# Sample attention of a hybrid decoder step in four 32-column strips, with a token-major norm and separate semaphores for key and value pages

## What is computed

```
def attn_sample(q, k, v, k_past, v_past, lam):
    s_past = jnp.einsum("bqhnd,bkhnd->bhnqk", q, k_past) * scale
    s_new = jnp.einsum("bqhnd,bkhnd->bhnqk", q, k) * scale      # causal among the 8 new tokens
    w = softmax(concat(s_past, s_new))[:, :, 0] - lam * softmax(...)[:, :, 1]
    return einsum(w[..., :p], v_past) + einsum(w[..., p:], v)
o = rmsnorm(o, subln) * (1.0 - lam_init)
```

## Time and profile before

| | us |
|---|---|
| median of three runs (3421.71 to 3428.89) | 3424.6 |
| the profiled execution: its own time | 3428.04 |
| its span | 3426.4 |
| TensorE busy | 3235.2 (94% of the span) |
| VectorE busy | 1520.3 (44%) |
| ScalarE busy | 1083.0 (32%) |
| mean granted TensorE clock | 0.955 |

### The profile page before, as it was taken

How to read it: one execution, slowest core, us unless ns; L and a number is a source line. 1 busy time by engine, 2 the same in 40 slices (tenths; PEclk the granted TensorE clock), 3 DMA queues, 4 the chain that set the end, 5 groups by cost and what they waited for, 6 DMA issues and landing times.

```text
span 3426.4 us, 56080 instructions
## 1 busy us (share of the span) xinstructions
PE 3235.2 (94%) x21279; PEld 2959.4 (86%) x21279; DVE 1520.3 (44%) x1994; ACT 1083.0 (32%) x1287; POOL 29.7 (1%) x55
## 2 busy tenths in 40 slices
PE   7899987997789999999999989999989999999998
PEld 2588853775778998998998989999989999999998
DVE  1534574113653443443433564445554444444443
ACT  1322233103333323323323333333343333333332
POOL 0000000000000000000000000000000000000000
PEclk8999996877899999999999989999999999999999
DMA  9777777662347557557567534444434444444443
GB/s 347 243 246 249 236 267 261 226 239 80 100 146 247 179 179 245 177 184 246 167 193 243 161 114 150 151 147 149 148 116 149 151 147 148 151 147 149 151 147 110
DMA packets 512217, 624.17 MB, mean 182 GB/s; under 512 B 22416, under 2 KB 408081, under 8 KB 511444
## 3 DMA queue, kind: packets, MB, share of 16 engines
q1 hardware_dynamic: 504576, 595.68, 54.5%
q0 software_dynamic: 6112, 22.84, 1.8%
q10 hardware_dynamic: 1430, 4.24, 0.4%
HBM read 617.13 MB, written 5.54 MB: 182 GB/s over the span
## 4 chain that ended last, share of the span: by engine, by line
PE 88%; DVE 4%; DMA 4%; ACT 1%; issue 1%; SPq 0%; POOL 0%; POOLq 0%; DVEq 0%; ACTq 0%
PE mm L1417 80%; PE aux L1417 7%; DMA wide_first<-in_ada_mix_w 2%; DMA vpage<-in_cache_v 2%; PE mm L1510 1%; DVE a_rr L1201 1%; DVE l_g L1308 0%; SPq L362 0%; ACT tmp L613 0%; DVE a_qn L1204 0%; DVE pj L1212 0%; DVE p_s L1228 0%; DVE a_t L1210 0%; DVE rstd L898 0%; DVE a_t L1208 0%
## 5 line engine op out<-in xcount | busy, mean ns | idle before, releaser
L844 DVE TENSOR_TENSOR w_lo<-raw,w_hi 128x1024 fp32r<-128x1024 f32 x752 | 920.2, 1226 | 1431.2 <-ACT w_hi L526 1429.4
L526 ACT ACTIVATE w_hi<-raw 128x1024 fp32r<-128x1024 f32 x752 | 795.4, 1059 | 1724.8 <-PE mm L1417 1724.8
L1417 PE MATMUL mm<-h_hi,w_hi 128*128 128x320 f32 x3712 | 1164.6, 314 | 54.2 <-DVE h_lo L940 32.3
L1417 PE MATMUL mm<-h_hi,w_lo 128*128 128x320 f32 x3712 | 1151.4, 310 | 0.0
L1417 PE MATMUL mm<-h_lo,w_hi 128*128 128x320 f32 x3712 | 1151.3, 310 | 0.0
L1417 PEld LDWEIGHTS mm<-h_hi,w_hi 128*128 128x128 f32 x3712 | 701.5, 189 | 135.8 <-issue 133.2
L1417 PE MATMUL mm<-u_hi,w_hi 128*128 128x320 f32 x2304 | 712.0, 309 | 0.0
L1417 PE MATMUL mm<-u_hi,w_lo 128*128 128x320 f32 x2304 | 711.9, 309 | 0.0
L1417 PE MATMUL mm<-u_lo,w_hi 128*128 128x320 f32 x2304 | 711.9, 309 | 0.0
L1417 PEld LDWEIGHTS mm<-h_lo,w_hi 128*128 128x128 f32 x3712 | 701.7, 189 | 2.2 <-issue 2.2
L1417 PEld LDWEIGHTS mm<-h_hi,w_lo 128*128 128x128 f32 x3712 | 701.1, 189 | 0.0
(11 more groups left out here) (247 smaller groups left out, 1448.2 us busy)
## 6 DMA issues: line engine op xcount, KB each, us to landing
raw<-in_mlp_w SPq DMA_DIRECT2D x512, 512.0 KB, 3.6
narrow<-in_ada_mlp_w SPq DMA_DIRECT2D x256, 256.0 KB, 3.6
raw<-in_w_in_odd SPq DMA_DIRECT2D x96, 512.0 KB, 3.6
raw<-in_w_in_even SPq DMA_DIRECT2D x80, 512.0 KB, 6.6
wide_first<-in_ada_mix_w SPq DMA_DIRECT2D x64, 512.0 KB, 8.8
narrow<-in_ada_mix_w SPq DMA_DIRECT2D x128, 256.0 KB, 3.7
wide_later<-in_ada_mlp_w SPq DMA_DIRECT2D x64, 512.0 KB, 6.0
wide_later<-in_ada_mix_w SPq DMA_DIRECT2D x64, 512.0 KB, 5.2
```

The costliest lines, as they stand in the source:

```text
L526: fn(w_hi[:, slot], raw[:, slot], ACT.Copy).then_inc(hi_ready, 1)
L844: v.tensor_tensor(w_lo[:, slot], raw[:, slot], w_hi[:, slot].bitcast(F32), ALU.subtract).then_inc(lo_ready, 1)
L1417: return nc.tensor.matmul(out, lhsT, rhs, start=first, stop=last)
```

## The change

It does these things:

1. **Scores in strips.** `s_q` is now [128, 8 heads, 32]: for head h = 2j + a the 16 query columns stand at column 16a of its 32, the rest is zero. Head h goes to the PSUM strip 32j, and the two heads of a strip add into it, so the rows of the scores keep their order. The stationary operand has 32 columns in place of 128. The matmuls on the new keys move ahead of `fold`, next to those on the past keys.
2. **Values in strips.** The weights `s_pt` are now stationary, 32 columns for four samples, and the value pages move, 128 columns a head. Head 4*half + j goes to strip 32j; the result in `aux[:, 0, :]` is token-major and adds up over the four samples of a group. Since the columns of the other samples must be zero, VectorE clears the eight of the sample before. `s_pt` moves to a place that was `ktok`, and VectorE clears it first, behind a wait for `stored`.
3. **Token-major norm.** ScalarE squares the four 128 x 128 blocks of the result with a running sum, takes the roots; VectorE multiplies; TensorE turns the four blocks back (`s_back`); VectorE puts them into `pj` behind the second head of the prompt's norm and only then counts `s_out`. The head norm runs on 256 columns instead of 320.
4. **Own semaphores.** Keys count `keys_in`, values `values_in`. The keys of sample b wait for the transposes of sample b - 2 (`s_kTt` >= 2b - 2), only the values for `s_o` >= b - 1. TensorE waits for `values_in` ahead of the values.

```diff
-                if b >= 2:
-                    pool.wait_ge(s_o, b - 1)
...
+                if b >= 2:
+                    pool.wait_ge(s_kTt, 2 * b - 2)
+                for g in range(PAGES):
+                    pool.dma_start((kpage, kpage2)[b % 2][:, g, :],
...
+                                   ).then_inc(keys_in[b % 2], 16)
                 if b >= 2:
                     pool.wait_ge(s_o, b - 1)
                 for g in range(PAGES):
...
+                    pool.dma_start((vpage, vpage2)[b % 2][:, g, :],
...
+                                   ).then_inc(values_in[b % 2], 16)
...
             act.wait_ge(s_o, NB)
-            fn(pj[:, 0:H, SEQ:T], aux[:, 0, :].rearrange("p (h t) -> p h t", h=H), ACT.Copy).then_inc(s_out, 1)
-            act.wait_ge(s_out, 1)
+            for n in range(4):
+                ins = fn(s_kT[:, n // 2, P * (n % 2):P * (n % 2) + P], aux[:, 0, P * n:P * n + P], ACT.Square,
+                         accum_out=small[:, 1, 8 + n:9 + n])
+            ins.then_inc(s_sq, 1)
+            act.wait_ge(s_sq, 1)
+            fn(small[:, 1, 12:16], small[:, 1, 8:12], ACT.Sqrt, scale=1.0 / DV, bias=C("eps")).then_inc(s_root, 1)
...
-            step(v.memset(s_q[:, :], 0.0))
+            step(v.memset(s_q[:, :, :], 0.0))
+            dve.wait_ge(stored, 64)
+            step(v.memset(s_pt[:, :, :, :], 0.0))
...
                 if b:
                     dve.wait_ge(s_o, b)
+                    v.memset(s_pt[:, :, :, before:before + 8], 0.0)
...
+            dve.wait_ge(s_root, 1)
+            step(v.reciprocal(small[:, 1, 12:16], small[:, 1, 12:16]))
+            settle()
+            v.tensor_tensor(s_kT[:, 2:4, :].rearrange("p a (n d) -> p (a n) d", n=2),
+                            aux[:, 0, :].rearrange("p (n d) -> p n d", n=4),
+                            small[:, 1, 12:16].unsqueeze(2).broadcast_to([P, 4, P]), ALU.mult).then_inc(s_norm, 1)
             for i in range(H):
...
+                if i == 1:
+                    dve.wait_ge(s_back, 1)
+                    for n in range(4):
+                        rows, cols = slice(4 * (n % 2), 4 * (n % 2) + 4), slice(SEQ + 32 * (n // 2), SEQ + 32 * (n // 2) + 32)
+                        ins = v.tensor_scalar(pj[:, rows, cols], mm[:, 0, 0, P * n:P * n + P].rearrange("p (j t) -> p j t", j=4),
+                                              subln[:, 0:1], None, ALU.mult)
+                    ins.then_inc(s_out, 1)
...
-                for h in range(H):
-                    mul(mm[:, 2, 0, 0:PAST], s_q[:, P * h:P * h + P], s_kT[:, h, :], h == 0, h == H - 1)
+                for a in range(2):
+                    for j in range(4):
+                        h = 2 * j + a
+                        mul(mm[32 * j:32 * j + 32, 2, 0, 0:PAST], s_q[:, h, :], s_kT[:, h, :], a == 0, a == 1)
...
                 pe.wait_ge(s_pte, b + 1)
-                for h in range(H):
-                    out, cols, w = aux[:, 0, 64 * h + 8 * b:64 * h + 8 * b + 8], slice(P * h, P * h + P), slice(8 * h, 8 * h + 8)
-                    mul(out, page[:, 0, cols], s_pt[:, 0, w], True, False)
-                    mul(out, page[:, 1, cols], s_pt[:, 1, w], False, False)
-                    ins = mul(out, vtok[0:TS, 2, cols], s_pt[0:TS, 2, w], False, True)
+                pe.wait_ge(values_in[b % 2], 32 * (b // 2 + 1))
+                for half in range(2):
+                    for k in range(3):
+                        rows = P if k < 2 else TS
+                        keys = page[:, k, :] if k < 2 else vtok[0:TS, 2, :]
+                        for j in range(4):
+                            h = 4 * half + j
+                            at_col = 256 * (b // 4) + P * half
+                            ins = nc.tensor.matmul(aux[32 * j:32 * j + 32, 0, at_col:at_col + P], s_pt[0:rows, k, h, :],
+                                                   keys[:, P * h:P * h + P], start=b == half == k == 0,
+                                                   stop=b == NB - 1 and k == 2, skip_group_check=True)
```

More of the change, by code:

```diff
@@ L232, in trunk_kernel @@
         s_kT = at("s_kT", RM, [P, H, PAST])
-        s_q = at("s_q", RM + 8192, [P, H * (P + 16)])
+        s_q = at("s_q", RM + 8192, [P, H, 32])
         s_s = at("s_s", RM + 12800, [P, T])
-        s_pt = at("s_pt", RM + 14080, [P, 3, 64])
+        s_pt = at("s_pt", RH + 8192, [P, 3, H, 32])
         l_x2 = at("l_x2", RM, [P, 2, T])
@@ L477, in _ @@
                     pool.wait_ge(stored, 64)
+                pages = []
+                for g in range(PAGES):
+                    n = b * PAGES + g
+                    pages.append(pool.value_load(ptab[0:1, n:n + 1], min_val=0, max_val=A["cache_k"].shape[1] - 1))
+                if b >= 2:
+                    pool.wait_ge(s_kTt, 2 * b - 2)
+                for g in range(PAGES):
+                    pool.dma_start((kpage, kpage2)[b % 2][:, g, :],
+                                   A["cache_k"][0, bass.ds(pages[g], 1)].rearrange("o p h d -> p (o h d)")
+                                   ).then_inc(keys_in[b % 2], 16)
                 if b >= 2:
@@ L480, in _ @@
                 for g in range(PAGES):
[L481 to L485, removed]
+                    pool.dma_start((vpage, vpage2)[b % 2][:, g, :],
+                                   A["cache_v"][0, bass.ds(pages[g], 1)].rearrange("o p h d -> p (o h d)")
+                                   ).then_inc(values_in[b % 2], 16)
             pool.wait_ge(s_out, 1)
@@ L761, in _ @@
             act.wait_ge(o_ready, H)
+            act.wait_ge(s_out, 1)
             def mixed(n):
@@ L1274, in s_keys @@
                     half = slice(DH * n, DH * n + DH)
-                    ins = v.tensor_copy(s_q[half, :].rearrange("p (h c) -> p h c", h=H)[:, :, 8 * n:8 * n + DS],
-                                        pj[half, 0:H, SEQ + DS * b:SEQ + DS * b + DS])
+                    for a in range(2):
+                        at_col = 16 * a + 8 * n
+                        ins = v.tensor_copy(s_q[half, a:H:2, at_col:at_col + DS],
+                                            pj[half, a:H:2, SEQ + DS * b:SEQ + DS * b + DS])
                 ins.then_inc(s_prep, 1)
@@ L1677, in _ @@
             pe.wait_ge(mod_ready, F.now)
+            pe.wait_ge(s_norm, 1)
+            for n in range(4):
+                ins = turn(mm[:, 0, 0, P * n:P * n + P], s_kT[:, 2 + n // 2, P * (n % 2):P * (n % 2) + P])
+            ins.then_inc(s_back, 1)
             for i in range(H):
@@ L1681, in _ @@
                     pe.wait_ge(o_root, i - 1)
-                mul(mm[:, 2, i % 2, 0:T], C("ones"), l_g[:, 0, i % 2], True, True).then_inc(o_ms, 1)
+                mul(mm[:, 2, i % 2, 0:SEQ], C("ones"), l_g[:, 0, i % 2, 0:SEQ], True, True).then_inc(o_ms, 1)
             pe.wait_ge(gate_in, 64)
```

33 lines of the change are left out of this document (20 added, 13 removed).

## The result

| | before | after |
|---|---|---|
| median, us | 3426.74 (4 runs, 3421.71 to 3429.55) | 3339.58 (4 runs, 3338.09 to 3341.93) |
| ratio | | 0.9749, 95% from 0.9734 to 0.9765 |
| profiled execution, us | 3428.04, span 3426.4 | 3340.85, span 3339.1 |
| granted TensorE clock, mean | 0.955 | 0.966 |
| sample attention, first scores to the end of the last burst | 605.38 to 814.6, 209.2 us | 607.04 to 719.6, 112.6 us |

A forecast was written before the change was run, and what follows sets the result against it. It took one loop, TensorE's sample plus a page load that cannot start earlier, as the bound. From 3428.0 us, less 79.5 for the stage, 0 behind it and half of 3.4, came 3347 us, range 3325 to 3385.

The forecast's parts named there:

- What bounds it now: Sample attention, 209 us for eight samples: bound by one loop, TensorE's sample plus a page load that cannot start earlier.
- Strips at once: Scores and values: four strips run at once, past-key scores 1.0 us, new-key scores 0.5, values 2.2 at full clock.
- The end of 5.8 us: Values in strips: 5.8 us if each record took the 0.12 us of the new-key scores before the change.
- rivals 2 and 3: Strips not running at once, about 3393 us, chance 0.05; each strip draining before the next, about 3570, chance 0.02.
- TensorE's sample: TensorE's steps for one sample of the attention stage, summed: 11.5 us at full clock, 20.3 at half clock.
- The clock: Sample attention: granted clock taken as 0.7, between full and half clock, so a TensorE sample takes 15.6 us.
- Rival 1: Sample attention: clock stays at 0.50, TensorE bounds each sample at 20.3 us, about 3380 us in all; chance 0.25.
- Own semaphores: Sample attention: the transposes' wait of 1.87 us for key pages goes in each of seven samples; adaLN chunks are late next.
- What the stage takes: Sample attention: 42.5 MB of chunks and pages plus start, tail and gaps; ends at 735 instead of 814.6, gain 79.5 us.
- I add 10 us: Sample attention: an allowance for gaps between loads, since TensorE takes chunks in bursts and the ring holds one group.
- At 370 GB/s: Sample attention: the rate assumed for the 42.5 MB of loads, which gives 115 us.
- Behind the stage: After sample attention: +3 us before the first head, heads at 2.15 us each, sum 0; gates' weights covered by 5 us.

The follow-up runs named there:

- x2: The kernel before with only `s_q` at 32 columns per head and both kinds of scores in strips ahead of `fold`: 3424.31 us, ratio 1.0005.
- x1: The kernel before with only the semaphores and the order of the page loads changed, all matmuls as before: 3417.31 us, ratio 0.998.
- x3: The changed kernel, but the keys of sample b wait for `s_o` >= b - 1 again, as the values do: 3356.59 us, ratio 0.9815.
- x4: The changed kernel with `s_q` and the scores as before, values in strips and own semaphores kept: 3347.81 us, ratio 0.9786.
- x5: The changed kernel without the 12 value page loads of samples 2 to 7, earlier pages multiplied again: 3320.64 us, ratio 0.9685.

## Why the prediction was right, point by point

**What bounds it now: right in the main.** A loop of TensorE's steps and a page load that starts too late. It is not TensorE's whole sample, as the prediction has it: the scores lie beside the load. x2 shows that (shorter scores alone give nothing), x1 shows the load (earlier pages alone give 13 us in the stage), and x3 and x4 price the two inside the change at 16 and 9. Alone they are worth 13 and 0, together with the value strips 96.6, and the value strips are the largest part (x3, x4).

**Strips at once: right.** Scores 1.1 us against a summed 1.5, values 2.1 against 2.2. The end of 5.8 us that the range held for the values, and rivals 2 and 3, fall with it.

**TensorE's sample: a little too high.** 11.5 us at full clock had been summed; sample 0 takes 9.4. Of the 2.1 us, 1.0 is `fold`, which sample 0 doesn't have, and 0.4 are scores. It costs nothing in the time, since the DMA is the longer.

**The clock: between the forecast's cases, nearer to its good end.** I took 0.7 and a TensorE sample of 15.6. The stage was granted 0.90. Windows of after behind its longest waits for `wide_later`, and between two of them:

```profile
630.00:640.00 10.00, 9.49 (x61) 5.88 (x62) 1.95 (x7) 1.25 (x3) 0.00 (x0) 0.51 1.04 399
...
657.00:664.00 7.00, 5.25 (x54) 2.41 (x52) 0.00 (x0) 0.00 (x0) 0.00 (x0) 0.52 1.05 390
664.00:687.00 23.00, 19.83 (x226) 11.10 (x218) 7.69 (x27) 4.55 (x8) 4.21 (x8) 1.00 1.04 395
688.00:694.00 6.00, 5.10 (x22) 1.89 (x26) 0.48 (x3) 0.00 (x0) 0.00 (x0) 0.50 1.05 387
```

The clock fell three times, each time behind such an idle stretch of TensorE: 3.4 us, 1.8 and 1.7 us one after the other, and 2.7 us. In x5, the same matmuls with no idle stretch over 1.2 us from the first scores to the last burst, it was never below 1.00. Rival 1, half clock throughout, falls with that. The Trainium skill, "TensorE: Matmul & The Clock Gate", section "HAM oscillation", has a kernel that is throttled at every wait for DMA, with waits longer than its bursts. The trace agrees for the longest waits here and not for the short ones.

**Own semaphores: right, the price in part by luck.** The transposes no longer wait, and the adaLN chunk is what is late next. The price of 7 x 1.9 us, 13, is x1's 12.6, but the trace of before has six such waits of TensorE, 10.4 us in all, since the first sample's transposes (611.7) have none.

**What the stage takes: the term that was mis-sized.** 42.5 MB at 370 GB/s plus 4, 4 and 10 us was to end at 735; it ended at 719.6. Two parts of the term failed, both to the same side. "I add 10 us" for gaps: there were none (DMA share 1.00). "At 370 GB/s": the steady part ran at 385 to 403, so the middle samples took 16.1 us on average instead of 17 to 18. 369 was the mean of 30 to 55 us of before; its first 19 us, at a DMA share of 1.05, already ran at 387, and the 416 of the earlier trace rows told the same. x5 confirms the rate by its pitch. The forecast counted 57 chunks from 602 us on; that count runs from 600, from 602 on there are 56.

**Behind the stage: sum nearly right, one part too high.** Timeline of after:

```profile
723.11 0.69 DVE L1330 TENSOR_TENSOR s_kT<-aux,small 128x512 f32<-128x512 f32 x1
...
726.43 1.75 DVE L1336 RECIPROCAL l_g<-l_g 128x256 f32<-128x256 f32 x1 [2.63 <-ACT l_g L770]
...
728.62 1.75 DVE L1336 RECIPROCAL l_g<-l_g 128x256 f32<-128x256 f32 x1
...
731.99 1.80 POOL L498 MEMSET wgate<- 128x2048 f32 x1 [34.52 <-DVE pj L1344]
```

From the last burst's end (719.6) to the first reciprocal are 6.8 us, where it was 4.9: +1.9 against a summed +3. The heads go at 2.19 us (728.62 - 726.43) against 2.15. From the last burst to ScalarE's gates it is 26.8 us instead of 27.6: -0.8 against 0. The clearing of `wgate` is 12.4 us behind the burst, within 1 us of the forecast, and the gate matmuls wait 0.6 us for the first weights, 7 us before ScalarE wants the gates: covered.

**What no step held.** 95.8 us of lead became 87.3 at untouched loops, by where TensorE's instructions fall. The forecast's 79.5 came nearer to the 87 than the mechanism deserved: the stage gave 97 by its own ends, 17 more than forecast, and half of that was given back. The forecast costed added and removed instructions by their time alone and said nothing of their number.

## What to carry to other kernels

When a loop is bound by a resource's round trip (a page that may be fetched only after the step that frees it), write down which steps stand in the round trip and which lie beside the load. Shortening one beside it buys waiting (the scores, x2: nothing); shortening one inside it pays at once (the values, x3: 80 us with the loads as late as before). Then price the stage by bytes at the rate of a stretch in which the queues are really full. After any change to a long program, compare the two traces at common instances of one instruction down to the end, not only in the stage that was changed: a gain can leak at loops that nobody touched. If TensorE shows a new "issue" stop at a loop's start, a few harmless instructions placed in an idle stretch ahead of it cost one run to try, and gave 14 us here; they have to be tried again after each later edit.

## What the runs showed that I had not expected

- The place of TensorE's code has a price: a second stop of 2.6 us from start to start at three loop starts in the changed kernel, none with 120 instructions more ahead of it, 2.2 to 2.3 us with 256 more. More than half of the price is the clock behind the stop (0.66 for 10 us at two of the three, where before has 1.00), not the stop. In x1 and in the changed kernel the stop ends equally long behind the fetched packet (1.3 to 1.5 us); in the changed kernel it begins earlier, in the middle of the burst. No run tried other paddings than 8, 120 and 256.
- The granted clock of the stage went by two things. Waiting: 0.90 in the changed kernel, 1.00 in x5 on the same matmuls with shorter waits. And the matmuls themselves: in sample 0 of before TensorE runs without a pause from 605.4 on and its clock falls to half clock at 621.3, in the middle of the values with 8 moving columns. With the values in strips and almost no waits, x4 has 1.00 (TensorE busy for 96% of the stage); in x2, at 0.65, both are at work and were not separated.
- One core moved 385 GB/s or more for some 90 us on end, with chunks and pages on two queues.
- The 24 matmuls of the values, 48 records of 128 columns in four strips with 32-column weight loads, take 2.1 us, 45 ns a record.
